# Four query tiles projected inside the normalisation stages, 512-column token projections, and a turned inverse in a two-layer decoder step

## The reference, cut to what matters

```
z, xbc, dt_raw, q, kv, gate = split_cols(h @ lp['w_in'], ...)         # layer 0: z 1024 columns, kv 768, gate 48
y_ssm = rmsnorm(y * silu(z), norm_w)

qkv, z, b_raw, a_raw, dil = split_cols(h @ lp['w_in'], ...)           # layer 1: dil = q, k, v of 1536 columns each
q = l2norm(qkv[:, :, 0]) * (GDN_HEAD_DIM ** -0.5); k = l2norm(qkv[:, :, 1])
amat = strictly_lower(kb @ k.T * decay)                                # per head and chunk of 64
tmat = inverse(I + amat)
u, w = tmat @ vb, tmat @ (kb * exp(gc))
```

## Time and profile before

| | us |
|---|---|
| median of 3 runs | 2959.62 (2958.86 to 2959.94) |
| profiled execution, its own time | 2959.93 |
| its span in the profile | 2958.1 |
| granted TensorE clock, mean | 0.935 |
| PE busy | 2639.9 |
| ACT / DVE / POOL busy | 950.8 / 1240.5 / 901.4 |

### The profile page before, as it was taken

How to read it: one execution, slowest core, us unless ns; L and a number is a source line. 1 busy time by engine, 2 the same in 40 slices (tenths; PEclk the granted TensorE clock), 3 DMA queues, 4 the chain that set the end, 5 groups by cost and what they waited for, 6 DMA issues and landing times. The chain is left out here.

```text
span 2958.1 us, 46930 instructions
## 1 busy us (share of the span) xinstructions
PE 2639.9 (89%) x19663; PEld 2394.3 (81%) x19663; DVE 1240.5 (42%) x2527; ACT 950.8 (32%) x1755; POOL 901.4 (30%) x453
## 2 busy tenths in 40 slices
PE   5878989998989999979978887989998888999998
PEld 5745878656889999978867787779996578999997
DVE  5754411576343222252655365541105453522224
ACT  3342231355342211152432343222214544311122
POOL 2241221133254333343343233313230004533331
PEclk9977999899999999989988898889999999999998
DMA  4202255451222222222201120112322262122221
GB/s 149 75 15 79 74 92 143 137 216 67 48 67 77 81 86 86 86 75 77 72 17 31 31 72 17 31 31 85 97 72 74 70 185 86 58 86 86 83 76 61
DMA packets 217568, 232.91 MB, mean 79 GB/s; under 512 B 40780, under 2 KB 186668, under 8 KB 216750
## 3 DMA queue, kind: packets, MB, share of 16 engines
q1 hardware_dynamic: 215278, 229.66, 25.5%
q10 hardware_dynamic: 2080, 0.25, 0.1%
HBM read 207.93 MB, written 48.35 MB: 87 GB/s over the span
## 5 line engine op out<-in xcount | busy, mean ns | idle before, releaser
L283 POOL TENSOR_TENSOR WRr<-WR,WH 128x2048 fp32r<-128x2048 f32 (+3 forms) x98 | 435.8, 4447 | 929.2 <-ACT WH L271 832.4
L2258 PE MATMUL PS<-HHr,WRr 128*128 128x288 f32 x1104 | 328.4, 297 | 0.0
L423 PE MATMUL PS<-HHr,WH 128*128 128x288 f32 (+1 forms) x928 | 282.8, 305 | 41.0 <-PEq L107 41.0
L423 PE MATMUL PS<-YTr,WRr 128*128 128x288 f32 x1024 | 304.0, 297 | 0.0
L271 ACT CAST WH<-WR 128x2048 fp32r<-128x2048 f32 (+3 forms) x98 | 180.3, 1840 | 335.8 <-DMA WR<-in_mlp_w 191.9
L423 PE MATMUL PS<-YTr,lt_WX 128*128 128x288 f32 x1408 | 281.8, 295 | 0.0
L423 PE MATMUL PS<-HTr,WH 128*128 128x288 f32 (+1 forms) x928 | 279.9, 302 | 0.0
L423 PE MATMUL PS<-HHr,WRr 128*128 128x288 f32 (+1 forms) x928 | 279.8, 302 | 0.0
L283 POOL TENSOR_TENSOR WRr<-WR,lt_WX 128x2048 fp32r<-128x2048 f32 x35 | 162.2, 4634 | 233.6 <-ACT lt_WX L271 233.6
L423 PE MATMUL PS<-WH,HHr 128*128 128x256 f32 (+3 forms) x760 | 219.5, 289 | 10.9 <-PEq L107 10.9
L423 PEld LDWEIGHTS PS<-YTr,lt_WX 128*128 128x128 f32 x1408 | 227.1, 188 | 0.1
(11 more groups left out here) (672 smaller groups left out, 6113.8 us busy)
## 6 DMA issues: line engine op xcount, KB each, us to landing
WR<-in_mlp_w SPq DMA_DIRECT2D x64, 1024.0 KB, 5.3
WR<-in_cd_w_in SPq DMA_DIRECT2D x34, 1024.0 KB, 5.4
out_dil_s<-in_cache_dil_kv SPq DMA_DIRECT2D x2, 7936.0 KB
WR<-in_ab_w_in SPq DMA_DIRECT2D x10, 1024.0 KB, 5.4
past_rows<-in_cache_nsa_kv SPq DMA_DIRECT2D x16, 256.0 KB, 3.4
WR<-in_ab_w_in SPq DMA_DIRECT2D x16, 256.0 KB, 4.3
WR<-in_nsa_ck_w SPq DMA_DIRECT2D x4, 1024.0 KB, 5.8
WR<-in_nsa_cv_w SPq DMA_DIRECT2D x4, 1024.0 KB, 5.4
```

The lines of the kernel that those rows point to most:

```text
L283: pool.tensor_tensor(K.WRr[:, n % RING, 0:used], K.WR[:, n % RING, 0:used], high_slot(K, i, used).bitcast(F32), ALU.subtract).then_inc(K.l ...
L423: last = pe.matmul(out, a, b, start=(n == 0), stop=(n == 3 * len(terms) - 1))
L2258: last = pe.matmul(out, a[:, k, c], h[:, k, x], start=(n == 0), stop=(n == 3 * KT - 1))
```

## The change

Three edits, with what they need around them.

1. Token-stationary projections stream 512 columns (304 for the last keys and values of layer 0) into a whole PSUM bank. A weight chunk keeps its size but is now half of the contraction by 512 columns: all 5 token tiles are multiplied by the first half into 5 banks, then by the second half into the same banks, and evacuated then. This holds for z, for keys and values of layer 0, and for dilated keys and values.
2. Two weight chunks, four of the twelve dilated query tiles, move into `gdn_l2norm`, one chunk a pass. ACT copies their results to a buffer `QE` and, at the start of the dilated query stage, from there to their place.
3. In `gdn_pair` levels 1 to 5 drop the product TXT. The transpose of the updated T is made by PE transposes one level later, between X and TX, and DVE copies it out in place of the subtraction.

```
+    def wide(w, c0, n):
+        for k0 in (0, KT // 2):
+            rows(w, k0, KT // 2, c0, n, TT)
...
+def wide_matmuls(K, pe, W, t, bank, half):
+    wh, wl = W
+    rows, n = TILES[t][1], wh.shape[2]
+    x = slice(t * P, t * P + rows)
+    kt = KT // 2
+    for k in range(kt):
+        h, l = K.HH[:, kt * half + k, x], K.HTr[:, kt * half + k, x]
+        for m, (a, w) in enumerate(((h, wh), (h, wl), (l, wh))):
+            last = pe.matmul(K.PS[0:rows, bank, 0:n], a, w[:, k, :], start=(half == 0 and k == 0 and m == 0),
+                             stop=(half == 1 and k == kt - 1 and m == 2), skip_group_check=True)
+    return last
...
 def gdn_l2norm(...):
         @block.sync
         def _(sp):
+            fill_ring(K, sp, chunk + RING)
             sp.wait_ge(kept_out, 3)
             store_conv_state(K, sp, rows, K.o_gdn_conv_p[0], K.o_gdn_conv_s[0], cols)
         @block.tensor
         def _(pe):
             turn_kept(K, pe, keep, 12).then_inc(kept_turned, 1)
+            W = split_wait(K, pe, chunk)
+            half_projection(K, pe, W, 0, 0, 0)
+            half_projection(K, pe, W, 0, 0, 1).then_inc(K.mm, 1)
+            half_projection(K, pe, W, 1, 1, 0).then_inc(q_half, 1)
+            half_projection(K, pe, W, 1, 1, 1).then_inc(K.mm, 1)
...
+            split_low(K, pool, chunk + 1)        # POOL, behind its four products
...
+            split_high(K, act, chunk + 1)        # ACT, behind the exponentials
+            act.wait_ge(K.mm, K.end[chunk] - 1)
+            act.copy(in_halves(QE[:, 0, :]), both_halves(K, 0)).then_inc(q_out, 1)
+            act.wait_ge(q_half, 1)
+            act.copy(QE[:, 1, half_of(0)], K.PS[:, 2, 0:HALF]).then_inc(q_out, 1)
+            act.wait_ge(K.mm, K.end[chunk])
+            act.copy(QE[:, 1, half_of(1)], K.PS[:, 3, 0:HALF]).then_inc(q_out, 1)
...
 gdn_pair, PE:
                     else:
-                        pe.wait_ge(dves[a], DV[("TT", k - 1)])
+                        pe.wait_ge(dves[a], DV[("TM", k - 1)])
                     tiles(b.A, b.AL, b.TM, n).then_inc(pes[a], 1)
+                if k > 1:
+                    for a, b in enumerate(B):
+                        turn(b.Bp, b.TM, TT if k < 4 else NT).then_inc(pes[a], 1)
                 for a, b in enumerate(B):
                     pe.wait_ge(acts[a], AC[("XS", k)])
+                    if k > 1:
+                        pe.wait_ge(dves[a], DV[("TT", k - 1)])
                     if k < LEVELS - 1:
                         tiles(b.Bp, b.TT, b.XS, n).then_inc(pes[a], 1)
-                for a, b in enumerate(B):
-                    tiles(b.A, b.XS, b.TT, n).then_inc(pes[a], 1)
+                    else:
+                        tiles(b.A, b.XS, b.TT, n).then_inc(pes[a], 1)
 gdn_pair, DVE:
-                    dve.wait_ge(pes[a], PE[("TXT", k)])
-                    dve.tensor_tensor(b.TT[:, 0:n], b.TT[:, 0:n], b.A[:, 0:n], ALU.subtract).then_inc(dves[a], 1)
+                    if k < LEVELS - 1:
+                        dve.wait_ge(pes[a], PE[("T", k)])
+                        dve.tensor_copy(b.TT[:, 0:n], b.Bp[:, 0:n]).then_inc(dves[a], 1)
+                    else:
+                        dve.wait_ge(pes[a], PE[("TXT", k)])
+                        dve.tensor_tensor(b.TT[:, 0:n], b.TT[:, 0:n], b.A[:, 0:n], ALU.subtract).then_inc(dves[a], 1)
```

More of the change, by code:

```diff
@@ L425, in split_products, with proj_matmuls, project @@
     return last
-def proj_matmuls(K, pe, W, mode, at, pair):
+def proj_matmuls(K, pe, W, at, pair):
     wh, wl = W
[L432 to L442, removed]
-    return last
-def project(nc, K, name, units, masks=None, sync=None, ahead=0):
+    c = slice(at * P, (at + 1) * P)
+    for b in range(2):
+        x = slice(b * HALF, (b + 1) * HALF)
+        last = split_products(pe, K.PS[:, 2 * pair + b, 0:HALF],
+                              [((wh[:, k, c], wl[:, k, c]), (K.HH[:, k, x], K.HTr[:, k, x])) for k in range(KT)])
+    return last
+def wide_matmuls(K, pe, W, t, bank, half):
[9 more added lines that the diff above has]
+    return last
+def project(nc, K, name, units, masks=None, sync=None, early=(), ahead=0):
     done_by = {"act": [0], "dve": [0]}
+    place, n_wide, n_pairs = [], 0, 0
     for u in units:
@@ L490, in evacuate @@
                     eng.wait_ge(K.mm, first + i + 1)
-                    evac(eng, i % 4, at).then_inc(sem[e], 1)
+                    evac(eng, place[i], at).then_inc(sem[e], 1)
         @block.scalar
         def _(act):
+            for out, held_q in early:
+                act.copy(out, held_q)
             evacuate(act, "act")
@@ L1406, in ssm_gate, with product_at @@
     with ExitStack() as ctx:
-        SZ = ctx.enter_context(nc.sbuf_tensor("g_SZ", [P, 2, QW], F32))
+        SZ = ctx.enter_context(nc.sbuf_tensor("g_SZ", [P, 2, WIDE], F32))
         masks = SampleMasks(nc, ctx, 3, ((0, 1),))
-        units = [(c, t) for c in range(4) for t in range(TT)]
-        before = K.end[chunk - 1]
+        units = [(c, t) for c in range(2) for t in range(TT)]
+        def product_at(c, t):
+            return K.end[chunk + 2 * c] + t + 1
         with stage(nc, "z_silu", "z_used") as (block, z_silu, z_used):
@@ L1423, in _ @@
             def _(pe):
[L1424 to L1429, removed]
+                for c in range(2):
+                    for half in range(2):
+                        W = split_wait(K, pe, chunk + 2 * c + half)
+                        for t in range(TT):
+                            i = TT * c + t
+                            if half == 0 and i >= 8:
+                                pe.wait_ge(z_silu, i - 7)
+                            wide_matmuls(K, pe, W, t, i % 8, half).then_inc(K.mm, 1)
             @block.scalar
@@ L3146, in tiles, with turn @@
                 return last
-            def turn(out, src):
-                for t in range(TT):
+            def turn(out, src, n=TT):
+                for t in range(n):
                     last = pe.transpose(tile_(out, t), tile_(src, t), K.ident[:])
@@ L3291, in dilated_keys @@
                 w = min(DIL_W[g], PAST)
-                stores.append([(K.o_dil_s[g][0, b, w - NS:, 0, cc].rearrange("s h d -> s (h d)"), b * NS, NS) for b in range(NB)])
+                stores.append([(K.o_dil_s[g][0, b, w - NS:, 0].rearrange("s h d -> s (h d)"), b * NS, NS) for b in range(NB)])
         @block.sync
         def _(sp):
-            for i, (c, t) in enumerate(units):
+            for i, (g, t) in enumerate(units):
                 if t == 0:
-                    fill_ring(K, sp, chunk + c - 1 + RING)
+                    fill_ring(K, sp, chunk + 2 * g + RING)
                 sp.wait_ge(k_rows, i + 1)
@@ L3302, in _ @@
                     K.n_keys_out[i % 4] += 1
[L3303 removed]
+                if t == 1:
+                    fill_ring(K, sp, chunk + 2 * g + 1 + RING)
         @block.gpsimd
@@ L3332, in _ @@
             sent = [0] * 4
-            for i, (c, t) in enumerate(units):
+            for i, (g, t) in enumerate(units):
                 if t == 0:
-                    split_high(K, act, chunk + c + 1)
-                n = TILES[t][1]
-                act.wait_ge(K.mm, before + i + 1)
+                    split_high(K, act, chunk + 2 * g + 1)
+                if t == 1:
+                    split_high(K, act, chunk + 2 * g + 2)
+                act.wait_ge(K.mm, K.end[chunk + 2 * g] + t + 1)
                 if i >= 4:
```

169 lines of the change are left out of this document (100 added, 69 removed).

## The result

The changed kernel took 2939.24 us (median of 5 executions, 2925.85 to 2941.26) beside 2959.94 for the kernel before (5 executions, 2958.86 to 2961.17): ratio 0.9919, 95% interval 0.9907 to 0.9932. That is 20.7 us off, where 47.5 were forecast (2912.4, with a range from 2901 to 2931). The kernel is faster, but by less than half of what was forecast, and the time lies above the range.

What follows compares the result with a forecast made beforehand. PE, busy 89% of the span, was taken as the bound: 2959.93 - 11.7 (wide columns) - 19.8 (moved query tiles) - 15.7 (inverse) = 2912.7 us, 2912.4 as median, range 2901 to 2931.

Steps and rivals of the forecast that it cites:

- part 3: Levels of the inverse in `gdn_pair`: transposes replace products, 3.9 us off a pair of heads, 15.7 us off in all.
- part 1: Projections z, keys and values: 512 columns remove 1080 matmuls at 12.1 ns, less later last copies, 11.7 us off.
- part 2: Query tiles moved into normalisation: 25.4 us off the query stage, 9.6 growth, 4.0 back, so 19.8 us off.
- The sum itself: Whole kernel: the three gains, 11.7, 19.8 and 15.7 us, taken off the profiled 2959.93 us, giving 2912.7.
- D: Levels of the inverse: the clock falls to 1.2 GHz, costing 80 us, total 2992 us; chance 0.06.
- The price of 118.75 ns: Value projection: one 256-column matmul from start to start, 12.1 ns of it independent of columns; 512 columns put at 225.4 ns.
- the 10 us: Normalisation stages: growth by more than 10 us would show the prediction wrong; 9.6 us was forecast.
- The return at the next stage's start: Start of `gdn_pair` after normalisation: PE may start at full clock, 2.0 us back a pass, 4.0 in all.
- Rival C: Normalisation stages: moved queries run wholly at the low clock, both stages grow by 14.4 us, total 2936; chance 0.10.
- Rival B: Levels of the inverse: a chain of waits, transposes dear as products or DVE's copy later, total 2922; chance 0.10.
- A: Wide projections: 512 columns cost twice 256 and pay nothing, total 2925 us; chance 0.07.
- E: Layer 0's 304-column chunks: PE waits for splits, at worst some 4 us, 2916; inside the forecast's range, chance 0.67 together.

Runs made afterwards that it cites:

- the two sets: The changed kernel, five executions on each of two chips, against the kernel before: 2939.24 us, ratio 0.9919, then 2933.78 us, ratio 0.9921.
- the edit alone: The kernel before with only the inverse's products replaced by transposes in `gdn_pair`: 2950.61 us, ratio 0.9973.
- the part alone: The kernel before with only the four query tiles moved into the normalisation stages and `QE`: 2940.87 us, ratio 0.9945.
- 6 extra: The changed kernel with the first matmul of layer 0's key/value projection issued 6 times more (512 columns): 2933.4 us.

## Why the prediction was wrong, by its steps

The sum was 47.2 us off the profiled execution. Between the profiled spans it was 28.8 (20.7 and 25.2 between the medians of the two sets). The 18.4 that are missing are 11.7 in untouched stages, 4.7 in part 3, 2.9 in part 1 and 1.1 in part 2, less 1.9 gained in all other stages. Another 8 us, between this profile's 28.8 and the first set's 20.7, lie between executions; no profile shows them, and their cause is open. By the table of stages:

- **The sum itself is the step that failed.** It added what changes inside the stages that are edited and took all others as fixed. The sample heads of layer 0 cost 6.9 us more and the dilated ones 4.8: 11.7 of the 18.4. For the first it is shown that the stage's start against the clock's changes decides, in both directions; for the second the cause is open. No rival named it: D looked for a falling clock inside the levels, where it stayed 1.00.
- **Part 3 was mis-sized**: 15.7 forecast. From the second head's X of level 1 to the product behind level 6 a pair took 31.50 us for 34.25, 2.75 off, 11.0 in four pairs; the edit alone gave 8.4 in all. Level 1 gave 2.24 of the 2.75 (2.34 forecast), levels 2 to 6 only 0.51 (1.58 forecast). The mechanism came as described, the wait of PE for the copy included (0.44 us for 0.57), but each level was 0.10 to 0.41 us longer than reckoned: behind each wait a group of products took 0.08 us more than the price used, and with 5 tiles DVE's longer subtraction and copy hold PE too. I kept the wait as given and never asked whether another order would hide it; that was worth 16.5 us in the levels and 12.0 in their stages.
- **Part 1 was mis-sized**: 11.7 forecast. The price of 118.75 ns is an average over two kinds. At 256 columns a matmul on a tile of 128 tokens costs 120.0 ns and one on the tile of 64 tokens 113.8 (mean distance of starts in the values stage at clock 1.00); at 512 columns they cost 226.8 and 230.0. So one wide matmul for two saves 13.2 ns on a full tile and loses 2.4 on the small one, 10.1 on average instead of 12.1. By such starts the four stages are worth about 11.1 us before the tails, an estimate, instead of 13.0. The stages gave 8.8 (1.8, -0.1, 2.8, 4.4). One stretch at 0.50 in the projections of layer 0 took back about 1.4 of it; against that, keys and values had 3.4 us less at 0.50 than before, worth about half of that. By "Back-to-back issue gap" of the page "TensorE: Matmul & The Clock Gate" in the Trainium skill the fixed part of an isolated matmul is 2.5 ns, which would make 2.7 us of the 1080, an estimate; the stages, with 8.8, and the 13.3 and 13.5 ns beside the columns on full tiles don't follow it.
- **Part 2 was right to 1.1 us**: 25.0 off the query stage for 25.4; growth 5.0 and 5.2 for 5.5 and 4.1, with SP last in both; the part alone gave 18.1 for 19.8. The growth hides two errors that nearly cancel: the second pass had 4.2 us at 0.50, its turns included, and PE busy for 16.1 us (15.4 forecast), the first 2.9 us and 15.6 (16.8). And the growth, 10.3 in all, is just over the 10 us that the prediction named as a sign of being wrong. The return at the next stage's start is small in the first pass and larger in the second: with this part alone the first pair stage grew by 1.0 us and the third shrank by 3.6, 2.6 together for 4.0. In the changed kernel the pair stages gave 15.0, 4.0 more than their levels. Rival C fails by the low clock: 2.9 and 4.2 us at 0.50 in the two stages, not all of the moved work.
- **Rival B**'s mechanism (PE waiting on DVE in the levels) took part, at 4.7 us of its 9.7. **D** fails: 44 of the 212 PE instructions in levels 2 to 6 are transposes, and the clock was 1.00 throughout. The same page of the Trainium skill says in "Part 4: PE-mode transpose" that full clock doesn't engage for transposes. The levels can't test that by themselves, since most of their work is products; the rise at 1771.9 behind twelve transposes alone goes against it, and what D made of it didn't come. **A** and **E** fail: the wide columns pay in their stages, and PE was busy 96.5 of the 97.7 us of the projections of layer 0, where E had it waiting for splits.

## What to carry to other kernels

An edit that saves a few us also moves every later stage against the changes of TensorE's clock. Here a stage where PE is busy three quarters of the time gained or lost a sixth of its length by that, so list such stages before summing, give each a term of both signs, and read a kernel's gain from its own stages as well as from the total. And where a new wait is found on paper, look for an order that hides it before pricing it: putting the transposes ahead of a product that does not need them took 16.5 us off levels in which the edit itself had saved 11.0.

## What the runs showed of the hardware

- The place of a stage in time, with its work unchanged, set its clock: the same 312 matmuls took 42.6 us in four kernels (before, the two with one part without wide columns, the changed one with 6 extra; the first fall of the clock 17.2 to 17.3 us in) and 49.4 to 50.3 us in all the others (2.7 to 3.3 us in).
- The place repeats where the code up to it is the same. In three kernels (before, moved tiles alone, inverse alone) the stage starts 713.6, 712.8 and 715.4 us into the span, and the first fall follows 17.27, 17.27 and 17.26 us later. In the seven with wide columns and no extra matmuls ahead of it, it starts between 706.7 and 712.8 us, and the fall follows 2.7 to 2.9 us later. So the start keeps its distance to the clock's changes and not to the kernel's own start; that earlier stages end on the clock's changes would explain it, but wasn't tested. The same page of the Trainium skill says, in "Part 1: The HAM clock gate", that the activity window is free-running and does not start with the kernel, which agrees: the clock's first fall comes 126.7 us into the span of one profile and 129.8 into that of another.
- Extra work made a stage shorter: 1.4 us more ahead, 6.8 us less in it.
- At full clock a pair of weight load and fp32r matmul costs 120.0 ns at 256 columns and 226.8 at 512 where 128 tokens are stationary (13.3 and 13.5 ns above the columns), and 113.8 and 230.0 ns where 64 are.
